# Ten picks tiles in place of eight: the spread of the expert layers starts two input tiles later

## The reference

```python
def peer_ffn(x, w_q, subkeys, u_tab, v_tab):     # for each block of 128 tokens
    q = (xb @ w_q).reshape(n, PEER_HEADS, 2, PEER_HALF)
    s = jnp.einsum('nhpc,pkc->nhpk', q, sk)      # scores against 2 x 128 sub-keys
    sv, si = lax.top_k(s, PEER_TOPK)             # 16 best of each half
    cand = sv[:, :, 0, :, None] + sv[:, :, 1, None, :]
    fv, fi = lax.top_k(cand, PEER_TOPK)          # 16 best pairs: expert = key0 * 128 + key1
    gw = jax.nn.softmax(fv, axis=-1)
    act = gelu(jnp.einsum('nhkd,nd->nhk', u_tab[eid], xb))
    return jnp.einsum('nhk,nhkd->nd', gw * act, v_tab[eid])
```

## Time and profile before

| | us |
|---|---|
| runs | 3249.74, 3243.47, 3247.17 |
| median | 3247.17 |
| profiled execution | 3245.87 |
| its span, first to last instruction | 3244.2 |
| PE busy in the span | 3097.2 |
| DVE busy | 2049.7 |
| ACT busy | 1233.2 |
| mean granted TensorE clock | 0.979 |

### The profile page before, as it was taken

The page is one execution under the profiler, slowest core; times in us unless marked ns, Lnnn a source line. Parts: engine busy times, 40 slices in busy tenths (PEclk is TensorE's granted clock), DMA queues, the critical chain, the costliest instruction groups (busy, mean ns, idle before and its releaser), DMA issues.

```text
span 3244.2 us, 52308 instructions
## 1 busy us (share of the span) xinstructions
PE 3097.2 (95%) x20148; PEld 2680.5 (83%) x20148; DVE 2049.7 (63%) x3700; ACT 1233.2 (38%) x1877; POOL 104.8 (3%) x133
## 2 busy tenths in 40 slices
PE   7989999999989999999999999999898999999999
PEld 3559999986689886888999999887687999999887
DVE  2566556544455522598966666785679985666687
ACT  1245445430444312322444444432531444444433
POOL 0200000000000000021000000000013000000000
PEclk9999999999989999999999999999899999999999
DMA  7444555542635532344666666674243566666674
GB/s 271 145 167 137 188 184 167 187 137 84 227 116 183 181 132 78 111 143 156 223 242 205 206 206 215 229 234 134 78 139 128 210 224 224 221 210 207 206 247 162
DMA packets 190666, 579.62 MB, mean 179 GB/s; under 512 B 16912, under 2 KB 61968, under 8 KB 185904
## 3 DMA queue, kind: packets, MB, share of 16 engines
q1 hardware_dynamic: 185552, 542.08, 49.4%
q10 hardware_dynamic: 4608, 33.56, 2.5%
q0 software_dynamic: 352, 1.90, 0.2%
HBM read 542.87 MB, written 34.60 MB: 178 GB/s over the span
## 4 chain that ended last, share of the span: by engine, by line
PE 84%; DVE 10%; ACT 3%; issue 1%; DMA 1%; PEld 0%; POOL 0%; SPq 0%; ACTq 0%; DVEq 0%; PEldq 0%; POOLq 0%
PE ps L1134 29%; PE ps L1212 28%; PE ps L928 5%; PE ps L875 3%; PE ps L1436 3%; PE ps L1413 3%; PE ps L931 2%; PE ps L1124 2%; DVE w_split L2414 1%; PE ps L1022 1%; PE ps L880 1%; PE ps L810 1%; DVE arena L2606 1%; PE ps L1007 1%; DVE arena L2600 1%
## 5 line engine op out<-in xcount | busy, mean ns | idle before, releaser
L2414 DVE TENSOR_TENSOR w_split<-ring,w_split 128x1024 fp32r<-128x1024 f32 (+1 forms) x707 | 865.9, 1226 | 613.1 <-ACT w_split L1858 612.4
L1134 PE MATMUL ps<-x_split,w_split 128*128 128x256 f32 x8352 | 1057.1, 284 | 24.7 <-DVE w_split L2414 18.9
L1134 PEld LDWEIGHTS ps<-x_split,w_split 128*128 128x128 f32 x8352 | 1037.6, 192 | 46.8 <-issue 22.3
L1858 ACT ACTIVATE w_split<-ring 128x1024 fp32r<-128x1024 f32 (+1 forms) x707 | 746.7, 1058 | 749.7 <-PE ps L1212 461.6
L1212 PE MATMUL ps<-w_split,h_split 128*128 128x512 f32 (+1 forms) x4056 | 958.8, 391 | 4.9 <-DVE w_split L2414 2.9
L1212 PEld LDWEIGHTS ps<-w_split,h_split 128*128 128x128 f32 (+1 forms) x4056 | 748.6, 188 | 154.5 <-DVE w_split L2414 5.2
L1918 ACT ACTIVATE arena<-ps 128x256 f32<-128x256 f32 (+1 forms) x256 | 98.3, 385 | 496.0 <-PE ps L1134 413.7
L928 PE MATMUL ps<-arena,ring 128*128 128x512 f32 (+1 forms) x416 | 152.7, 524 | 4.7 <-ACT arena L1688 4.0
L1413 PE MATMUL ps<-x,ring 128*128 128x256 f32 x608 | 136.8, 381 | 0.0
L928 PEld LDWEIGHTS ps<-arena,ring 128*128 128x128 f32 x416 | 81.3, 196 | 67.1 <-issue 60.7
L875 PE MATMUL ps<-x,ring 128*128 128x256 f32 (+1 forms) x608 | 133.1, 381 | 0.3 <-DVE x L2357 0.3
(11 more groups left out here) (297 smaller groups left out, 2408.5 us busy)
## 6 DMA issues: line engine op xcount, KB each, us to landing
ring<-in_peer_u SPq DMA_DIRECT2D x256, 512.0 KB, 3.4
ring<-in_peer_v SPq DMA_DIRECT2D x256, 512.0 KB, 4.2
ring<-in_ffn_in SPq DMA_DIRECT2D x132, 512.0 KB, 3.2
ring<-in_ada SPq DMA_DIRECT2D x96, 512.0 KB, 5.4
ring<-in_ffn_out SPq DMA_DIRECT2D x66, 512.0 KB, 3.2
spread_rows<-arena ACTq DMA_DIRECT2D x32, 1024.0 KB, 3.9
arena<-spread_rows SPq DMA_DIRECT2D x20, 1536.0 KB, 8.5
ring<-in_pq SPq DMA_DIRECT2D x32, 512.0 KB, 3.3
```

Of the source, the lines that this page charges most:

```text
L1134: last = mm(dst, w_split[:, w, wp, at:at + P], rhs[rp], start=(first and i == 0), stop=(final and i == 2), skip_group_check=shared)
L1858: f(w_split[0:rows, w, 0, :], ring[0:rows, slot, :], ACT.Copy).then_inc(w_high, 1)
L2414: v.tensor_tensor(w_split[0:rows, w, 1, :], ring[0:rows, slot, :], w_split[0:rows, w, 0, :].bitcast(F32), ALU.subtract).then_inc(w_low, 1)
```

## The change

`U_PICK` goes from 8 to 10. The spreads stand before tiles 26 to 57 in place of 24 to 55, and two tiles (58, 59) in place of four lie behind the tile of the last one. The turn of the picks and the copy that follows it have their offsets changed so that they stay before tile 21 and at tile 22. The list of plain tiles was 0, 16 to 23, and 24, 27, ..., 54; it becomes 0, 16 to 25, and 27, 30, ..., 57: 22 tiles in place of 20.

```diff
-U_PICK, U_SPREAD = 8, 32
+U_PICK, U_SPREAD = 10, 32
 EARLY = 2 * QUERIES + (AHEAD - QUERIES)
 PLAIN = [u for u in range(AHEAD) if u < 1 or QUERIES <= u < QUERIES + U_PICK or QUERIES + U_PICK <= u < QUERIES + U_PICK + U_SPREAD and u % 3 == 0]
@@ TensorE, peer
                 for u in range(QUERIES, AHEAD):
-                    if u == QUERIES + U_PICK - 3:
+                    if u == QUERIES + U_PICK - 5:
                         turn_picks()
@@ ScalarE, peer
-                    if u == QUERIES + U_PICK - 2:
+                    if u == QUERIES + U_PICK - 4:
                         for t in range(2):
                             act.wait_ge(k_turn, 2 * lb + t + 1)
```

## The result

The changed kernel takes 3255.7 us (median of 9 runs, 3251.65 to 3259.96), the kernel before 3247.17 us beside it. The ratio is 1.0031 with a 95% interval of 1.0022 to 1.0039, so 7 to 13 us slower. One of the nine runs of the kernel before was a slow one of 4641.56 us, which the ratio leaves out. Forecast was 3257, slower, by 9.5 us.

What follows compares the result with a forecast made beforehand. TensorE was taken as the bound (84% of the span). Delays of 3.3 and 3.2 us plus 2 x 1.5 us of clock made 9.5: 3255.4 from the profiled 3245.87, so a median of about 3257, range 3250 to 3264.

Steps and rivals of the forecast that it cites:

- Bound and place: TensorE sets the pace; loss expected behind the last spread, where cover behind the store shrinks by 5.2 us a layer.
- the 2 to 5 us forecast: TensorE's idle time before its first output product in both layers, released by VectorE's low part of the first output block.
- First and last spread: First spread 6.7 us later; intervals up to the last 0.6 us shorter in all; last spread 6.0 to 6.1 us later.
- the clock at the turn: After TensorE's wait at the turn, about 2.8 us of work at half speed, 1.4 us lost, read from the earlier trace.
- VectorE's lead: Before the first spread, VectorE has both hot buffers filled when TensorE comes; this covers a wait taken as 0.3 us.
- the rival of a faster loop: If VectorE paced the spread loop, 0.25 us saved on every spread would give 3241 us or less; chance 0.04.
- The store: Last store of spread rows: ordinary landing, about 3.9 us, taken as likelier in layer 2 than the trace's 6.56 us.
- a late one: Instruction packet on the last store: one layer late gives 3260 us (chance 0.24), both layers 3263 (0.06).
- The read and the block: Behind the last store: read and first output block, both coming 6.0 us later along with the last spread.
- The clock behind the idle time: At the output products after TensorE's idle time: granted clock falls to 0.50, costing 1.5 us a layer (ends 0 and 2.4).
- The sum: First output product 3.3 us later in layer 3, 3.2 in layer 2, plus 2 x 1.5 us of clock: 9.5 us.
- The wait at the turn: TensorE's 6.13 us wait for VectorE's last reduction at the turn of the picks, claimed to stay unchanged.

Runs made afterwards that it cites:

- The move alone: Kernel before with the spreads two tiles later and the old list of plain tiles; 3255.31 us, ratio 1.0029.
- the list alone: Kernel before with tiles 25 and 57 made plain and the spreads left where they were (also called list only); 3250.28 us, ratio 1.0014.
- taking one transfer out of the path: Changed kernel with the first output block and input block fetched ahead of SyncE's wait for the stores; 3250.7 us, ratio 1.0013.
- early block in the kernel before: Kernel before with the first output block and input block fetched ahead of SyncE's wait for the stores; 3244.91 us, ratio 0.9999.
- the later turn: Changed kernel with the turn of the picks before tile 23 and its copy at tile 24, two tiles later; 3252.55 us, ratio 1.0020.
- the exponential was moved: Changed kernel with the turn two tiles later, plus ScalarE's exponential of the pick weights at tile 21 instead of 19; 3238.86 us, ratio 0.9984.

## Why the prediction was right or wrong

**Bound and place: right.** The loss sits where it was put, between the last spread and the first output product. The move alone brings a ratio of 1.0029 of the 1.0031, the list alone 1.0014, and taking one transfer out of the path gives more than half of the loss back. The idle times of 2.81 and 3.33 us lie in the 2 to 5 us forecast, with the releaser named.

**First and last spread: right but for the clock at the turn.** I had the first spread 6.7 us later after the turn; it was 8.25 and 7.50. The ten traced layers with five plain tiles there and the turn at its old place gave 20.06 to 21.72 us, the six with three 13.40 to 15.08. The least of each differ by 6.66, the sum's term; the rest is the time in which the clock comes back, up to 1.7 us of scatter in either kernel, which the sum left out. First to last spread went from 143.81 to 143.16 us: -0.65, forecast -0.6. VectorE's lead gave nothing, and the rival of a faster loop is out.

**The store: right, for a reason that I did not have.** Both last stores landed in the ordinary 3.8 us. I had called a late one a matter of chance, and it is not: it goes by the place in the program. In layer 2 the last store took 6.5, 5.7 and 5.7 us to land in the three traces with the spreads at their old place (before, list only, early block in the kernel before), each with one packet of the instruction queue (q8) some 2.3 us behind its issue. In the traces with ten tiles whose read waits for the stores it took 3.8 us, with no such packet on it. The twelve traces with that wait hold 384 stores of spread rows. Into the first 3 us of 94 of them starts a packet of q8: each of these landed after 4.68 us or more, with a median of 5.35. The median of the other 290 is 3.88, with 37 of them over 4.4. So the move took layer 2's last store off the packet. Which stores get a packet stays much the same in the traces with ten tiles, whatever their shift in time. A row on where these packets fall would have borne on the chances of a late store, which I took from one layer of each kind.

**The read and the block: a term was missing.** From the read's issue to ScalarE's start on the block it took 8.38 and 8.18 us before (1664.69 to 1673.07 in the earlier trace rows), and 8.63 and 9.16 after. I had taken it as unchanged. The difference is in the read: from its issue to VectorE's weighting it took 7.06 and 6.87 us before, 7.35 and 7.81 after, and the block follows 1.3 us later in all four. SyncE now finds more slots of the ring free and issues six blocks in the 5 us behind the read, where it issued five and four before; that these slow the read is likely, and was not tried by itself.

**The clock behind the idle time: right in size.** I took 1.5 us a layer, and it was 1.55 in both. I had put the drop into the idle time; in layer 2 it came between 1 and 2 us after work had begun again, in layer 3 at once. That it came in both layers was likely and not certain: of the eleven traced layers with 2.4 us or more of idle time there, two (3.36 and 3.18 us) show no drop, and two others lost 2.7 us.

**The sum.** Layer 3 was to be 3.3 us later at the first output product and was 5.2: 0.8 by the clock at the turn, 1.0 by the read. Layer 2, 3.2 against 5.2: 1.6 at the turn, 0.3 at the read. The rest, 0.1 to 0.2 us, is rounding in the sum. With the clock, the change's own part of the two traces is 2 x (5.2 + 1.55) = 13.5 us, against 9.5 forecast and 7 to 13 measured. 2.4 of the 13.5 are the clock at the turn, which was at the short end of its scatter in both layers of the trace before; without them it is 11.1. The other stretches scatter as much. From the sixty-first output product of layer 2 to the turn of layer 3 the nine traces with the same code there show 493.0 to 497.1 us, 496.1 before and 494.3 after. So the mechanism and its terms were right, the missing ones (read and clock at the turn) make the sum too small by 1.6 to 4 us, and that the median came within 1 us of the forecast difference is partly luck.

**The wait at the turn stayed, and what it hid.** That it would not move was right. That plain tiles could fill it was assumed in the expectation for the later turn, and was wrong until the exponential was moved.

## What to carry to other kernels

Work moved ahead of a chain of dependent transfers is taken from the cover behind it. Before moving a stage, add up the path from its last instruction (store, landing, read, first block, split) and the work that runs beside it. In layer 2 of the kernel before both started at the last spread, at 1655.82; the path let the first output product start at 1675.53 and TensorE's own work ended at 1675.47, so 19.7 us stood against 19.7. And when a wait of one engine is to be filled, ask what the engine that empties its banks is doing meanwhile: a second wait can hide under the first.

## What the runs showed of the hardware

- After the same 6.13 us wait the clock stayed at 1.2 GHz for 2.8 us of work in one trace and for 6 us in another. The same code from turn to first spread took 13.4 to 15.1 us, and 11.97 us where there was no wait and the clock stayed at 2.4 GHz. This alone moves an execution by up to 1.7 us a layer.
- The length of an idle time did not decide alone whether the clock fell. Ahead of the first output product it fell around nine of eleven idle times of 2.4 us or more, among them 2.47 and 2.55 us, and not around the other two, of 3.18 and 3.36 us. It fell in none of the layers with 1.6 us or less. The fall came during the idle time in some layers and up to 1.5 us behind it in others, and cost 1.5 to 1.6 us in seven layers and 2.7 us in two.
- Dropping the wait between a 1 MB store and a 1.5 MB read brought a 0.5 MB block behind them 1.7 us sooner in one layer and 0.8 us in the other, not 4: 10.85 us in place of 12.52, 12.26 in place of 13.03.
- A 1 MB store landed in 3.88 us (median of 290), and in 5.35 us (median of 94) when a 16 KB packet of the instruction queue started in its first 3 us. In the traces with ten tiles these packets fall on nearly the same stores; in those with eight, on others. Moving a stage changes which stores they hit. That the packet is what delays the store is the plain reading, and no run took the packets away.
